# The attention mask: added to the bias by GpSimd instead of to the logits by TensorE

## The reference

```
score = sum_h w[t,h] * relu(q_idx[t,h] . k_idx[s])      # an indexer; s <= t
sel   = the 128 keys with the highest score of each query
logits = q . k / 8 + rel_bias[bucket(t - s), head]      # selected keys only
p      = softmax(logits) over the selected keys;  out = p @ v
```

## Time and profile before

| | us |
|---|---|
| median of 3 runs | 560.7 (559.05 to 562.09) |
| profiled execution | 562.05 |
| its span | 560.3 |
| PE busy | 536.4 (96%) |
| DVE busy | 369.9 (66%) |
| ACT busy | 235.1 (42%) |
| POOL busy | 263.7 (47%) |

### The profile page before, as it was taken

The page is one execution under the profiler, slowest core; times in us unless marked ns, Lnnn a source line. Parts: engine busy times, 40 slices in busy tenths (PEclk is TensorE's granted clock), DMA queues, the critical chain, the costliest instruction groups (busy, mean ns, idle before and its releaser), DMA issues.

```text
span 560.3 us, 7405 instructions
## 1 busy us (share of the span) xinstructions
PE 536.4 (96%) x2789; PEld 425.7 (76%) x2791; DVE 369.9 (66%) x751; ACT 235.1 (42%) x356; POOL 263.7 (47%) x136
## 2 busy tenths in 40 slices
PE   5899999999998899999999997999999999999995
PEld 5776888778776778787888885877777677788884
DVE  2694599648778345555460057599989999738825
ACT  4543743233311234453361335255655655156413
POOL 3380555755531053033006324469999997351601
PEclk9799999999999789999999997999999999989999
DMA  6264354321222021000162503222222222302004
GB/s 230 41 178 163 101 167 145 90 68 71 75 76 77 0 76 61 15 2 1 32 269 77 138 13 112 81 70 76 76 76 75 76 79 89 134 0 76 1 1 150
DMA packets 44653, 46.75 MB, mean 83 GB/s; under 512 B 4426, under 2 KB 33117, under 8 KB 44617
## 3 DMA queue, kind: packets, MB, share of 16 engines
q1 hardware_dynamic: 44616, 46.28, 26.2%
HBM read 44.03 MB, written 2.12 MB: 82 GB/s over the span
## 4 chain that ended last, share of the span: by engine, by line
PE 79%; DVE 10%; ACT 3%; issue 3%; POOL 2%; DMA 2%; SPq 1%; POOLq 0%; ACTq 0%; DVEq 0%
PE bank L1364 32%; PE bank L1384 27%; PE bank L1614 3%; PE bank L1555 3%; DVE r_va L965 3%; PE bank L1481 3%; DVE top L963 2%; PE bank L1531 2%; DMA w_raw<-in_w_in_even_dram 2%; PE bank L1544 2%; DVE r_ob L949 1%; PE bank L1620 1%; POOL w_lo L507 1%; PE bank L1493 1%; ACT hT_hi L622 1%
## 5 line engine op out<-in xcount | busy, mean ns | idle before, releaser
L507 POOL TENSOR_TENSOR w_lo<-w_raw,w_hi 128x2048 fp32r<-128x2048 f32 (+1 forms) x35 | 158.4, 4529 | 187.7 <-ACT w_hi L617 187.7
L1364 PE MATMUL bank<-hT_hi,w_hi 128*128 128x512 f32 (+1 forms) x312 | 127.7, 409 | 0.5 <-POOL w_lo L507 0.3
L1364 PE MATMUL bank<-hT_lo,w_hi 128*128 128x512 f32 (+1 forms) x312 | 125.2, 401 | 0.0
L1364 PE MATMUL bank<-hT_hi,w_lo 128*128 128x512 f32 (+1 forms) x312 | 124.6, 403 | 0.0
L1384 PE MATMUL bank<-w_hi,hT_hi 128*128 128x512 f32 x256 | 105.0, 410 | 0.0
L1384 PE MATMUL bank<-w_hi,hT_lo 128*128 128x512 f32 x256 | 100.9, 394 | 0.0
L1384 PE MATMUL bank<-w_lo,hT_hi 128*128 128x512 f32 x256 | 100.8, 394 | 0.0
L617 ACT ACTIVATE w_hi<-w_raw 128x2048 fp32r<-128x2048 f32 (+1 forms) x35 | 65.6, 1878 | 44.8 <-PE bank L1384 37.0
L1191 DVE SCALAR_TENSOR_TENSOR bank<-r_va,pvec,bank 128x512 f32<-128x512 f32 x108 | 76.1, 753 | 0.9
L1364 PEld LDWEIGHTS bank<-hT_hi,w_hi 128*128 128x128 f32 (+1 forms) x312 | 59.9, 192 | 17.2 <-issue 3.7
L1364 PEld LDWEIGHTS bank<-hT_lo,w_hi 128*128 128x128 f32 (+1 forms) x312 | 59.7, 191 | 15.6 <-issue 3.2
(11 more groups left out here) (189 smaller groups left out, 691.9 us busy)
## 6 DMA issues: line engine op xcount, KB each, us to landing
w_raw<-in_w_in_even_dram SPq DMA_DIRECT2D x14, 1024.0 KB, 5.2
w_raw<-in_w_in_odd_dram SPq DMA_DIRECT2D x16, 512.0 KB, 4.6
w_raw<-in_w_out_even_dram SPq DMA_DIRECT2D x4, 1024.0 KB, 8.3
w_raw<-in_w_in_odd_dram SPq DMA_DIRECT2D x4, 1024.0 KB, 5.1
w_raw<-in_w_out_odd_dram SPq DMA_DIRECT2D x4, 1024.0 KB, 5.1
r_x<-in_x_dram SPq DMA_DIRECT2D x4, 512.0 KB, 4.8
r_x<-bias_rows SPq DMA_DIRECT2D x4, 512.0 KB, 6.2
r_x<-in_x_dram SPq DMA_DIRECT2D x1, 2048.0 KB, 7.9
```

The lines of the kernel that those rows point to most:

```text
L507: nc.gpsimd.tensor_tensor(v(w_lo[j % 3]), v(w_raw[j % 2]), v(w_hi[j % 3]).bitcast(F32), ALU.subtract).then_inc(lo_ready, 1)
L1364: ins = nc.tensor.matmul(proj_bank(g)[0:m, :], w[:, k, P * i:P * i + m], h[:, k, :], start=(n == 0), stop=(n == 3 * KC - 1))
```

## The change

PE's mask matmuls go, and q.k starts its banks itself. POOL adds the mask to the bias row by row of a new tile, masked (two buffers, in a part of r_g that is free by then), one tile per step; DVE's logits take this tile instead of the bias. In slots 12 to 15 POOL's split of slot s+2 is cut in four quarters of 512 columns, with two mask tiles ahead of each.

```
+            def quarter_lo(j, i):
+                cols = slice(512 * i, 512 * i + 512)
+                if i == 0:
+                    pool.wait_ge(hi_ready, j + 1)
+                    wait_slot_used(pool, j - 3)
+                ins = nc.gpsimd.tensor_tensor(w_lo[j % 3][:, cols], w_raw[j % 2][:, cols],
+                                              w_hi[j % 3][:, cols].bitcast(F32), ALU.subtract)
+                if i == 3:
+                    ins.then_inc(lo_ready, 1)
+
+            def masked_bias(n):
+                tb, h = divmod(n, AH)
+                w = P * (tb + 1)
+                if n == 0:
+                    pool.wait_ge(fill_done, LAST_FILL[1] + 1)
+                    pool.wait_ge(table_in, 16 * len(TABLE_HEADS))
+                if tb and h == 0:
+                    pool.wait_ge(mask_ready, tb)
+                if n >= 2:
+                    pool.wait_ge(logit_ready, n - 1)
+                nc.gpsimd.tensor_tensor(masked[n % 2][:, 0:w], bias_cols(h, w), neg_mask[:, MASK_AT[tb]:MASK_AT[tb] + w],
+                                        ALU.add).then_inc(masked_ready, 1)
...
-                if s_ + 2 < NS and s_ != 2:
+                if ATT_S0 <= s_ < S_OE:
+                    for i in range(4):
+                        n = AH * (s_ - ATT_S0) + 2 * i
+                        masked_bias(n)
+                        masked_bias(n + 1)
+                        quarter_lo(s_ + 2, i)
+                elif s_ + 2 < NS and s_ != 2:
                     split_lo(s_ + 2)
...
+                dve.wait_ge(masked_ready, n + 1)
                 nc.vector.tensor_tensor_reduce(out=logit[n % 2][:, 0:w], in0=bank[4 + n % 2][:, 0:w],
-                                               in1=bias_cols(h, w), scale=1.0, scalar=-3.0e38, op0=ALU.add,
+                                               in1=masked[n % 2][:, 0:w], scale=1.0, scalar=-3.0e38, op0=ALU.add,
...
-            dve.wait_ge(table_in, 16 * len(TABLE_HEADS))
...
-                if tb and h == 0:
-                    pe.wait_ge(mask_ready, tb)
-                for i in range(2):
-                    nc.tensor.matmul(bank[4 + i][:, 0:w], ident_bf[:], neg_mask[:, MASK_AT[tb]:MASK_AT[tb] + w],
-                                     start=True, stop=True)
...
-                                               kaT[64 * i:64 * i + 64, h // 2, c0:c1], start=False, stop=True,
-                                               skip_group_check=True)
+                                               kaT[64 * i:64 * i + 64, h // 2, c0:c1], start=True, stop=True)
```

More of the change, by code:

```diff
@@ L225, in hybrid_trunk @@
         probT = [r_g[:, 2048 + 512 * i:2560 + 512 * i] for i in (0, 1)]
+        masked = [r_g[:, 3072 + 512 * i:3584 + 512 * i] for i in (0, 1)]
         sq_b = [r_att[:, 512 * i:512 * i + 512] for i in range(TB)]
@@ L322, in hybrid_trunk @@
         max_ready = sem("max_ready")
+        masked_ready = sem("masked_ready")
         prob_ready = sem("prob_ready")
```

## The result

The changed kernel takes 574.75 us (median of 6 runs, 568.36 to 576.97), the kernel before 560.38 (559.05 to 562.09): ratio 1.0234, 95% interval 1.0178 to 1.029. A second series gave 575.83 against 560.63, ratio 1.0258 (1.0207 to 1.0309). The forecast was 568.6 with a range of 562 to 577: the direction and the mechanism are right; the loss is 14.4 us where 8.2 were forecast (7.9 by the prediction's own sum, which stood on 560.7). Medians here are over all executions of a series, ratios and intervals over its fast ones.

What follows compares the result with a forecast made beforehand. PE was taken as the bound, busy 536.4 of 560.3 us. Net waits 4.4, clock 3.0 and DVE collisions 0.5 sum to 7.9 us on the profiled 562.05, less 1.35 to the median: 568.6 us, range 562 to 577.

Steps and rivals of the forecast that it cites:

- The masks: PE in the attention: removing 32 mask matmuls saves 5.8 us, all on the chain, if nothing takes their place.
- POOL's tiles: POOL in the attention: mask tile additions take 0.46, 0.74, 1.02 and 1.29 us for the four widths.
- The wait behind quarter 0: Starts of slots 12 to 15: tile n0+2 queues behind quarter 0, which waits for ACT's w_hi; PE 8.6 us late.
- lateness: PE's delay at the slot starts: 0.7, 1.9, 5.2 and 0.8 us in slots 12 to 15, sum 8.6 us.
- The net of waits and masks: Attention: 8.6 us of lateness less 4.2 us of true gain from later pairs' masks, net +4.4 us.
- DVE against POOL: DVE products with two SBUF inputs in steps 10 to 13 and 20 to 23 collide with POOL; adds 0.5 us.
- The clock: PE after slot 14's stall: the clock falls to 0.50 for 6 us, losing 3.0 us; slots 13 and 15 left out.
- a rival with chance 0.15: Rival 1: clock falls in slots 13 and 15 (or 12) too, 3 us each, or double-price tiles; 572 to 577; chance 0.15.
- The rival that made them 3.2 us: Rival 2: four DVE and POOL collisions of 0.8 us ahead of PE; about 571.5 us; chance 0.08.
- That nothing comes back later: After the attention PE runs dense matmuls without waits, so nothing later takes the net +4.4 us back.
- faster (0.07): Rival 4: POOL is ahead everywhere in the attention and the masks' 5.8 us come home; 554.9 us; chance 0.07.
- no change (0.13): Rival 3 and its like: half-price tiles, no clock drop; about 563.3 us or less; rival 3's chance 0.12, outcome 0.13.

Runs made afterwards that it cites:

- e1: Kernel before without the 32 mask matmuls on PE and nothing in their place (mask left out of the computation); 555.18 us, ratio 0.991.
- e6: Changed kernel with 85 small matmuls on PE ahead of the transpose of step 17, filling slot 14's gap; 571.03 us, ratio 1.0179.
- e7: Changed kernel with only the quarters moved back by one pair of tiles in POOL's order; 554.98 us, ratio 0.991.
- second profile: Profile of the unchanged changed kernel run again beside the kernel before (series 575.83 us, ratio 1.0258); its profiled execution took 574.59 us.
- e4: Changed kernel with tiles one pair of steps earlier on POOL and quarters later; 554.43 us, ratio 0.9905; repeat 554.89 us, ratio 0.9899.
- e2: Changed kernel with PE's masks put back and DVE reading the bias, without its waits for POOL's tiles; 559.33 us, ratio 0.9991.
- e5: Changed kernel with ACT's split of slot 16 ahead of the gates' silu instead of behind it; 570.47 us, ratio 1.0185.
- e8: Changed kernel with the quarters moved behind tiles n0 to n0+5 in slot 14 alone; 564.13 us, ratio 1.0068.

## Why the prediction was right, and where its size was off

**The masks** (5.8 us forecast): 5.1 by the medians of e1, 4.3 in its trace. Right within the interval; by the trace 1.5 us too high. The price was read from the start of a mask to the start of its q.k; what a pair loses without its mask is less, 1.37 us for three pairs at 512 columns (27.53 against 26.16 in slot 15) where 0.53 each were counted.

**POOL's tiles** (0.46, 0.74, 1.02, 1.29 us forecast): 0.43, 0.67, 0.92 and 1.17. No price of the bf16 operand or of the reversed one shows (1.17 us, where the quarter of the same width takes 1.27). Right, 7 to 11% high.

**The wait behind quarter 0**: each link of the chain stands in the profile as forecast. For slot 14, counted from the end of w_hi: logits(18) forecast to begin 2.4 us after it (239.77 to 242.2), seen 243.46 - 241.08 = 2.4 us; the gap ahead of the transpose forecast almost 5 us, seen 5.06. e6, which has the wait without the low clock, takes 28.92 us in slot 14, 5.6 over e7's 23.30; forecast were 5.2 of lateness and 0.4 of eaten mask. Slot 15 is 1.9 us over e7 where its clock stays up (1.3 forecast). Slots 12 and 13 have no profile without a low clock; taking off the part that was lost, they are some 0.9 (second profile against e4's repeat, 19.59) and 2.2 over e7's order (0.9 and 2.2 forecast). The net of waits and masks over the attention was forecast as +4.4 us; it is 5.7 to 6.0 in the two profiles by the sum of 1 - granted. Right, a little small, and most of what is missing is the price of the masks, which were counted as 5.8 instead of 4.3.

**DVE against POOL** (0.5 us): the collisions happen, 2.2 us of DVE in e2, and cost PE nothing (e2 ratio 0.9991). The rival that made them 3.2 us falls. The rule of the Trainium skill (SBUF — State Buffer, Who interferes with whom) that such instructions contend agrees with the single ones: in e2 0.68 us became 1.03 in the mean for one group of four and 0.88 for the other, and 1.52 at most.

**The clock**: this is the term that was mis-sized. Slot 14's fall was forecast at 3.0 us and costs 3.2 and 2.2 us in the two profiles. What was wrong is that I left the other slots out of the sum, and gave them to a rival with chance 0.15. The runs show falls after gaps of 1.3 to 1.9 us too, in some executions and not in others. In the second profile, whose time is the typical one, slots 13 and 15 take 1.6 us more than in the first, in which less of the clock was lost there, and in e5 and e6, where the clock falls after slot 12's gap too, that slot takes 2.9 us more than in either. The at 193 us had shown that a gap of 1 us with another just before it is enough; I gave more weight to the dense matmuls between the stalls, and that was wrong. e8 says it from the other side: the three small starts cost 9.2 us, of which lateness (0.7 + 1.9 + 0.8) and the masks eaten (0.20 + 0.31 + 0.53) explain 4.4; the rest, 4.8 us, I put down to the clock. That is argued from e8's difference and from the slots of the profiles; no run isolates it for these slots as e6 does for slot 14.

**That nothing comes back later**: right in the second profile (12.5 us at the end of the attention, 12.6 in the span).

**Rivals**: faster (0.07) and no change (0.13) are out; the one with more of the clock was the case that came. 574.75 us lies in the stated range because that rival, to which I had given 0.15, stretched it; the forecast itself missed by 6 us.

## What to carry to other kernels

A helper engine with time to spare in the mean can still stop the bound engine, if short work that is wanted soon is queued behind an instruction that waits for a slow producer. When work is given to an in-order queue, walk it for each item: what waits ahead of it, who is queued behind its consumer. Here the same work in an order that lets the urgent tiles pass first turned a loss of 2.3% into a gain of 1.0%.

Where PE is the bound, count a gap not at its length alone but with the clock that may fall behind it, also where it is short: here gaps of 1.3 to 1.9 us were enough in some executions. In this kernel the waits are 10 to 11 of the 19.8 us between the two orders, and the clock most of the rest. The time scatters with it: 568.36 us at a mean granted clock of 0.970, 576.71 at 0.956, where the six times of the kernel before spread over 3.0 us.

## What the runs showed of the hardware

The same gaps, to 0.02 us, left the clock up in one execution and down in another. Slot 15's of 1.27 us in the first profile was followed by 1.00, its 1.26 us in the second by 0.50; slot 12's of 1.90 us in the first profile by 1.00, its 1.88 us in e5 by 0.50 from 200 to 204 us. Or the low stretch was longer: slot 13's gap of 1.55 us was followed by 0.62 and 0.52 from 218 to 222 us in the first profile, its 1.56 us by four whole microseconds of 0.50 in the second. Apart from the short gaps that follow on one another at 193 us, the shortest gap that a fall followed is 1.25 us (slot 15 in e5). And two executions of one kernel may differ before any change: from 185 to 189 us the first profile of the changed kernel had the full clock, while the kernel before had 0.50 from 183 to 186 with the same wait ahead of it:

```profile
185.00:189.00 4.00, 3.65 (x36) 2.98 (x32) 1.83 (x5) 0.00 (x0) 0.00 (x0) 1.00 0.00 0
```
```profile
183.00:186.00 3.00, 3.00 (x16) 2.99 (x15) 0.85 (x2) 0.00 (x0) 0.00 (x0) 0.50 0.00 0
```
